# Values and two probability tiles per head turned by 32 x 32 blocks and a trip through memory, in a two-layer encoder kernel

## The chip, the cores and the metric

The kernel runs on one core of a Trainium2 chip. The metric is the device time of one launch in microseconds (us), the median of three runs. The engines are TensorE (PE, with its weight loads as PEld), VectorE (DVE), ScalarE (ACT), GpSimd (POOL) and SyncE (SP), which here only issues DMAs and waits for semaphores. HBM is called memory below.

## The reference, cut to what matters

Two layers of an encoder for 512 prompt tokens and 64 sample tokens with 128 cached ones. Layer 0 has sixteen heads: 0 to 7 ("mla") and 8 to 15 ("diff", two softmax maps a head). Layer 1 has eight, 16 to 23 ("dsa", over the keys that an indexer selects). Keys and values of the heads 8 to 23 are outputs too, one row a token.

```python
q_lat, kv_lat, kpe_raw, dq, dk, dv = jnp.split(h @ w_in, SPLIT_EVEN, axis=-1)
...
logits = jnp.einsum('bqhmd,bkhmd->bmhqk', q, k2) * DIFF_SCALE + bias
p = jax.nn.softmax(jnp.where(mask, logits, -jnp.inf), axis=-1)
attn = (p[:, 0] - lam * p[:, 1]).astype(v.dtype)
return jnp.einsum('bhqk,bkhd->bqhd', attn, v)
...
# layer 1: q, k, v of a head likewise; softmax over the selected keys, p @ v
return mixed @ w_out, new        # new: dk, dv (and k, v of layer 1) are returned
```

Everything is float32. A product is made of three matmuls of parts (high x high, high x low, low x high): ACT writes the high part of an operand, DVE or POOL the low one.

## The kernel before

Tokens lie along the free dimension: a projection gives a tile of 128 features x 576 tokens. Each engine runs its own program, written out by hand, and semaphores hold them together. `attention(h)` of every engine goes through the slots 0 to 7 of head `h`. In the slots 0 to 4 PE makes the scores of the query tiles t = 0 to 3 (128 queries, 128 (t + 1) keys) and of the sample (t = 4); all slots hold a share of the projections q, k and v of a later head (of h + 1, in layer 1 of h + 2) as k-tiles of six matmuls, and some hold tiles of the output projection of a finished pair of heads. The slots of such heads are long (heads 9, 11, 13, 19, 21 from slot 0, heads 8, 11, 13, 18, 20 from slot 4); heads 10, 12, 14 and 17 have none, and 22 and 23 have only such tiles.

- **Probabilities.** DVE adds bias to the scores (`row_maxima`), ACT exponentiates and scales, in a diff head DVE mixes both maps. In slot t + 2 PE turns the tile by t + 1 transposes into a bank of T (`turn_probs`), ACT takes the high part into PTh (`turned_hi`), DVE the low part into PTl (`turned_lo`).
- **Values.** In slot 1 PE turns the five tiles of values to tokens (`values_to_tokens`), DVE copies them into VF (`take_values`), SP stores VF as output in slot 4 (`store_keys`), ACT and POOL split it into Vh and Vl (`job("v", h)`, slot 4, for head 23 slot 3).
- **Keys** are stored in another way: DVE turns 32 x 32 blocks into KF (`take_keys`, in slot 7 of the head before), and eight DMAs (four quarters of the prompt, four of the sample) write runs of 32 floats to the output.
- **Weighted values.** `weighted_values(h - 1)` stands in slot 1 of head h, right behind the value transposes.

PE accumulates into pairs of banks (SHORT and LONG uses); a group may open when DVE has taken what was last in its pair. In an even diff head, the rows for a per-head norm go through the LONG pair in slot 7, and `b_norm` on DVE frees it; the next head's q begins in it. Weights come in units of 512 KB into four buffers: SP loads, ACT makes the high part, POOL (or DVE) the low one. SP issues all of it in one order: `load_next("slot", h, s)` at the end of every slot, and a DMA waits behind every wait ahead of it.

Of the kernel before, what the change touches and what calls it, by code (L numbers as in the profile page):

```python
# [30 lines left out]
P = 128  # L31
# [12 lines left out]
HEADS = 8  # L44
# [271 lines left out]
def build(nc, a, outs, scratch):  # L316
# [58 lines left out]
    def plan_attention(h):  # L375
# [5 lines left out]
        for s in range(SLOTS):  # L381
# [5 lines left out]
            if 2 <= s < 2 + TOK_TILES and (h, s) != (16, 6):  # L387
                tr.add("p", h, s - 2)
# [4 lines left out]
            if s == 1:  # L393
                tr.add("v", h)
                tr.add("v5", h)
                if h % 16:
                    group("pv", h - 1, use=SHORT)
# [324 lines left out]
    with ctx:  # L722
# [54 lines left out]
        RSTDQ = sb("RSTDQ", [P, NT])  # L777
        arena = cursor[0]
# [47 lines left out]
        assert e <= own  # L826
        (QIh, QIl), end3 = overlay(end3, ("QIh", [P, 4, NT], F32R), ("QIl", [P, 4, NT], F32R))
# [67 lines left out]
        keys_made = sem("keys_made")  # L895
# [12 lines left out]
        pt_hi = sem("pt_hi")  # L908
        b_sq, rb_sqrt = sem("b_sq"), sem("rb_sqrt")
# [115 lines left out]
        def _(sp):  # L1025
# [99 lines left out]
            def store_keys(g):  # L1125

                sp.wait_ge(keys_made, g - HEADS + 1)
                dst = ("diff_k", "dsa_k")[kind_of(g) == "dsa"]
                c = slice((g % HEADS) * HD, (g % HEADS + 1) * HD)
                for name, b0, b1 in (("_prompt", 0, SEQ // SQUARE), ("_sample", SEQ // SQUARE, NT // SQUARE)):  # L1130
                    tokens = outs[dst + name][:, c].rearrange("(b t) (q d) -> q t b d", t=SQUARE, d=SQUARE)
                    for q in range(QUADRANTS):
                        sp.dma_start(tokens[q], KF[q * SQUARE:(q + 1) * SQUARE, b0:b1, :]).then_inc(kf_out, 16)
                sp.wait_ge(t_free, tr.made("v5", g))
                dst = ("diff_v", "dsa_v")[kind_of(g) == "dsa"]
                sp.dma_start(outs[dst + "_prompt"][:, c].rearrange("(t p) d -> p t d", p=P), VF[:, 0:QT, :]).then_inc(vf_out, 16)
                sp.dma_start(outs[dst + "_sample"][:, c], VF[0:DEC, QT, :]).then_inc(vf_out, 16)

# [89 lines left out]
            sp.wait_ge(vf_out, 16 * 2 * 16)  # L1228
# [42 lines left out]
        def job_source(name):  # L1271

            w = name[0]
            if name == ("ckv", KLT - 1):
                return acc_free, acc.made("krow")
            if w in ("kpe", "ckv"):
                return lat_ready, jobs.made(*name)
            if w == "qi":
                return acc_free, acc.made(*name)
            g = name[1]  # L1280
            if w in ("q", "k") and g == 17:
                return y_made, Y_MADE[w]
# [145 lines left out]
        def _(pe):  # L1428
# [209 lines left out]
            def values_to_tokens(h):  # L1638
                out = rotate_to_tokens(("v", h))
                if h == 17:  # L1640
                    pe.wait_ge(y_made, Y_MADE["v"])
                else:
                    pe.wait_ge(acc_free, acc.made("v", h))
# [60 lines left out]

            def turn_probs(h, t):
# [83 lines left out]
            def attention(h):  # L1789
                g, x = prepared_in(h), next_head(h)  # L1790
                for s in range(SLOTS):
# [12 lines left out]
                    if 2 <= s < 2 + TOK_TILES and (h, s) != (16, 6):  # L1804
                        turn_probs(h, s - 2)
                    if s == 1:
                        values_to_tokens(h)
                        if h % 16:
                            weighted_values(h - 1)
# [392 lines left out]
        def _(act):  # L2202
# [123 lines left out]
            def exponents(h, t):  # L2326
                kind, r, w = kind_of(h), rows_of(t), keys_of(t)
                n = step_of(h, t)
                if n >= 2:
                    act.wait_ge(t_done, tr.made("p", *divmod(n - 2, TOK_TILES)))  # L2330
# [24 lines left out]

            def b_square(h):
# [11 lines left out]
            def attention(h):  # L2368
                g, x, p = prepared_in(h), next_head(h), finished_pair(h)
                for s in range(SLOTS):  # L2370
# [6 lines left out]
                    if 2 <= s < 2 + TOK_TILES and (h, s) not in ((15, 5), (16, 4)):  # L2377
                        turned_hi(h, s - 2)
# [411 lines left out]
        def _(dve):  # L2790
# [235 lines left out]

            def take_values(h):
# [3 lines left out]
                if h > 8:  # L3031
                    dve.wait_ge(vf_out, 16 * 2 * stored_before(h))
# [45 lines left out]
            def mix_maps(h, t):  # L3078
# [5 lines left out]
                                         op0=ALU.mult, op1=ALU.add).then_inc(p_mixed, 1)  # L3084

# [72 lines left out]
            def attention(h):  # L3158
                g, x, p = prepared_in(h), next_head(h), finished_pair(h)
                for s in range(SLOTS):  # L3160
# [3 lines left out]
                    if s < TOK_TILES:  # L3164
                        row_maxima(h, s)
                    if h == 16 and s < 3:
# [6 lines left out]
                    if s == 1 and h != 16:  # L3173
# [5 lines left out]
                    if 2 <= s < 2 + TOK_TILES:  # L3179
                        turned_lo(h, s - 2)  # L3180
                    if s == 4 and h in (10, 12, 14, 15):
# [260 lines left out]
            def ffn(layer):  # L3442
# [4 lines left out]
                dve.wait_ge(vf_out, 16 * 2 * HEADS * (layer + 1))  # L3447
# [581 lines left out]
```

## Time and profile before

| | |
|---|---|
| median of three runs | 1642.27 us (1641.88 to 1643.78) |
| profiled execution | 1643.9 us, of it the span 1642.1 us |
| PE, PEld busy | 98%, 95% |
| DVE, ACT, POOL busy | 73%, 55%, 55% |
| share of the 16 DMA engines, main queue | 30.1% |
| granted PE clock, mean | 0.997 |
| stretch of heads 8 to 15 | from 263.8 us |
| stretch of heads 16 to 23 | from 1016.2 us |

Times in the trace are microseconds from the start of the span. The busy share of PE is high because matmuls are pipelined and overlap in the records: what an instruction costs is the distance from its start to the next one's. An engine's idle time costs only where another waits for it.

### The profile page before, as it was taken

To read this page: it belongs to the slowest core of one execution; us is meant where nothing else is said; L and a number is where in the kernel's file an instruction comes from. 1 tells how busy PE (TensorE), PEld (TensorE's weight loads), DVE (VectorE), ACT (ScalarE), POOL (GpSimd) and SP (SyncE) were. 2 spreads that over 40 slices of the span, in tenths; PEclk is the share of its full clock that TensorE was granted. 3 is DMA by queue.
4 is the path that set the end of the run, shared out by engine and by line. 5 is a ranking of instruction groups with operands and counts; after the bars stand their busy time and mean duration, and the time that the engine had idled before them with its cause. 6 is when DMAs were issued, how large, how long until landed. Compare 5 with 4: busy or idle time off the path is not lost.

```text
span 1642.1 us, 32437 instructions
## 1 busy us (share of the span) xinstructions
PE 1612.4 (98%) x12028; PEld 1563.2 (95%) x12028; DVE 1202.8 (73%) x2233; ACT 902.5 (55%) x1776; POOL 903.1 (55%) x703
## 2 busy tenths in 40 slices
PE   9999999999999999999999999999999999999998
PEld 8989999999999999999999999899999999999997
DVE  5666655656656799889897789634357998898977
ACT  4365545454546665565565445644367655655654
POOL 4453445364544067677575547664450676775754
PEclk9999999999999999999999999999999999999999
DMA  6221223343422223423323332344242233233232
GB/s 189 81 64 53 67 78 86 77 108 77 112 75 68 65 78 92 115 71 111 97 84 90 89 81 70 92 120 110 64 110 60 78 94 112 74 107 98 84 91 71
DMA packets 283008, 145.50 MB, mean 89 GB/s; under 512 B 60591, under 2 KB 273261, under 8 KB 282853
## 3 DMA queue, kind: packets, MB, share of 16 engines
q1 hardware_dynamic: 278392, 136.27, 30.1%
q0 software_dynamic: 3616, 6.92, 1.6%
q8 instruction: 98, 1.61, 0.4%
q14 instruction: 58, 0.47, 0.1%
q10 hardware_dynamic: 844, 0.24, 0.1%
HBM read 130.69 MB, written 15.32 MB: 89 GB/s over the span
## 4 chain that ended last, share of the span: by engine, by line
PE 81%; DVE 11%; ACT 3%; issue 3%; POOL 1%; DMA 0%; POOLq 0%; ACTq 0%; DVEq 0%
PE ACC L1444 29%; PE ACC L1883 11%; PE ACC L1884 11%; PE ACC L1885 11%; PE ACC L1724 2%; PE S L1699 2%; PE S L1885 2%; PE S L1883 2%; PE S L1884 2%; DVE SCO L3137 2%; DVE TOP L3134 1%; PE T L1444 1%; ACT PR L2335 1%; PE T L1712 1%; PE S L1673 1%
## 5 line engine op out<-in xcount | busy, mean ns | idle before, releaser
L3645 POOL TENSOR_TENSOR WL<-RAW,WH 128x1024 fp32r<-128x1024 f32 (+3 forms) x89 | 187.8, 2114 | 147.2 <-ACT WH L2210 147.0
L1444 PE MATMUL ACC<-XGh,WH 128*128 128x288 f32 (+1 forms) x1008 | 227.6, 307 | 6.3 <-DVE XGl L2828 1.8
L1444 PE MATMUL ACC<-XGh,WL 128*128 128x288 f32 (+1 forms) x1008 | 215.3, 295 | 0.0
L1444 PE MATMUL ACC<-XGl,WH 128*128 128x288 f32 (+1 forms) x1008 | 215.3, 295 | 0.0
L1883 PE MATMUL ACC<-TB,WH 128*128 128x288 f32 x640 | 188.5, 295 | 1.4 <-DVE TB L3355 1.4
L1885 PE MATMUL ACC<-TB,WL 128*128 128x288 f32 x640 | 188.6, 295 | 0.0
L1884 PE MATMUL ACC<-TB,WH 128*128 128x288 f32 x640 | 188.3, 294 | 0.0
L2493 ACT ACTIVATE TC<-ACC 128x288 f32<-128x288 f32 x192 | 79.0, 411 | 167.7 <-PE ACC L1885 167.0
L1444 PEld LDWEIGHTS ACC<-XGh,WH 128*128 128x128 f32 (+1 forms) x1008 | 159.0, 188 | 11.4 <-issue 4.0
L1444 PEld LDWEIGHTS ACC<-XGh,WL 128*128 128x128 f32 (+1 forms) x1008 | 161.6, 188 | 0.0
L1444 PEld LDWEIGHTS ACC<-XGl,WH 128*128 128x128 f32 (+1 forms) x1008 | 161.3, 187 | 0.0
L2335 ACT ACTIVATE PR<-SX,STAT 128x128 f32<-128x128 f32 (+4 forms) x160 | 85.7, 536 | 119.4 <-DVE STAT L3065 117.6
L2822 DVE TENSOR_TENSOR X<-ACC,X 128x576 f32<-128x576 f32 x89 | 66.7, 753 | 83.8 <-PE ACC L1444 79.4
L2210 ACT ACTIVATE WH<-RAW 128x1024 fp32r<-128x1024 f32 (+4 forms) x127 | 116.3, 923 | 12.9 <-PE S L1444 4.5
L1883 PEld LDWEIGHTS ACC<-TB,WH 128*128 128x128 f32 x640 | 120.2, 188 | 1.8 <-issue 1.8
L3308 DVE TENSOR_TENSOR WL<-RAW,WH 128x512 fp32r<-128x512 f32 (+3 forms) x128 | 120.4, 941 | 2.0 <-ACT WH L2511 2.0
L1884 PEld LDWEIGHTS ACC<-TB,WH 128*128 128x128 f32 x640 | 120.5, 188 | 0.0
L1885 PEld LDWEIGHTS ACC<-TB,WL 128*128 128x128 f32 x640 | 120.3, 188 | 0.0
L2511 ACT ACTIVATE WH<-RAW 128x1024 fp32r<-128x1024 f32 (+3 forms) x128 | 100.5, 787 | 34.4 <-PE S L1885 34.4
L3652 POOL TENSOR_TENSOR Ql<-YQ,Qh 128x576 fp32r<-128x576 f32 x24 | 34.9, 1455 | 112.2 <-ACT Qh L2241 112.1
L2351 ACT ACTIVATE PTh<-T 128x128 fp32r<-128x128 f32 (+1 forms) x96 | 41.2, 429 | 99.1 <-PE T L1712 98.8
L1883 PE MATMUL ACC<-XGh,WH 128*128 128x288 f32 x320 | 94.3, 295 | 0.0
(517 smaller groups left out, 5244.2 us busy)
## 6 DMA issues: line engine op xcount, KB each, us to landing
RAW<-in_w_gate_dram SPq DMA_DIRECT2D x44, 512.0 KB, 3.9
RAW<-in_w_up_dram SPq DMA_DIRECT2D x44, 512.0 KB, 5.0
RAW<-in_w_down_dram SPq DMA_DIRECT2D x48, 384.0 KB, 3.8
RAW<-in_w_in_even_dram SPq DMA_DIRECT2D x29, 512.0 KB, 5.2
RAW<-in_w_in_odd_dram SPq DMA_DIRECT2D x28, 512.0 KB, 4.6
RAW<-in_w_out_even_dram SPq DMA_DIRECT2D x16, 512.0 KB, 4.2
RAW<-in_w_down_dram SPq DMA_DIRECT2D x16, 256.0 KB, 2.9
RAW<-in_w_out_odd_dram SPq DMA_DIRECT2D x8, 512.0 KB, 5.1
```

Source lines behind the costliest of these rows:

```text
L1444: ins = pe.matmul(out[0:m, 512 * b:512 * b + width], left, right[:, b * width:(b + 1) * width], start=(first and part == 0), stop=(last an ...
L1883: pe.matmul(out, hi[:, w], xh, start=first and k == 0, stop=False, skip_group_check=not first)
L1884: pe.matmul(out, hi[:, w], xl, start=False, stop=False, skip_group_check=not first)
L1885: ins = pe.matmul(out, lo[:, w], xh, start=False, stop=k == count - 1, skip_group_check=not first)
L2210: act.activation(WH[slot][:, 0:n], RAW[slot][:, 0:n], ACT.Copy).then_inc(w_hi, 1)
L2335: act.activation(PR[m][0:r, n % 2, 0:w], SX[m][0:r, 0:w], ACT.Exp, bias=STAT[0:r, n % 2, m:m + 1], scale=-1.0, accum_out=STAT[0:r, n % 2, ...
L2351: act.activation(PTh[:, 0:t + 1, t * P:(t + 1) * P], out[:, 0:(t + 1) * P].rearrange("p (j q) -> p j q", q=P), ACT.Copy).then_inc(pt_hi, 1)
L2493: act.activation(dst, sum_bank(j), ACT.Copy).then_inc(copy_done, 1)
L2511: act.activation(blocks_of(layer, what, w)[0], src, ACT.Copy).then_inc(s7_hi, 1)
L2822: return lambda out: dve.tensor_tensor(two(X[:, m, :]), halves(out), two(X[:, m, :]), ALU.add)
L3308: dve.tensor_tensor(lo, src, hi.bitcast(F32), ALU.subtract).then_inc(s7_lo, 1)
L3645: pool.tensor_tensor(WL[slot][:, 0:n], RAW[slot][:, 0:n], WH[slot][:, 0:n].bitcast(F32), ALU.subtract).then_inc(w_lo_pool, 1)
```

## The change

Values of the heads 8 to 15 and 17 to 23 (`blockwise`) are no more turned by PE. DVE turns their 32 x 32 blocks into VT (`turn_values`, slot 0, for head 17 slot 1), SP stores VT by eight DMAs as it does the keys (slot 4 of its order, right behind them), waits after slot 7 until they have landed, and loads the stored output back into VF by two DMAs (`load_values`); `job("v", h)` waits for that.

The probability tiles t = 2 and 3 of the heads 8 to 14 and 17 to 22 (`BLOCK_HEADS`) are no more turned by PE either: DVE turns their blocks into PB (`probs_to_blocks`, slot t + 1), SP writes PB in four DMAs to a place in the memory of y_prompt and loads it back turned, by one DMA into PF (`turn_through_memory`, after `load_values`; between tile 2 and tile 3 stand the weight loads of slot 0 of the next head). ACT and DVE split PF (`loaded_hi`, `loaded_lo`: tile 2 in the slots 5 and 6, tile 3 in slot 7 of both, on DVE ahead of `b_norm` and of the end of v's projection). `weighted_values(h)` waits for the last of them.

Where slot 1 has an unfinished projection (the heads 9 to 14 and 17 to 21), `weighted_values(h - 1)` now stands behind the first of its three k-tiles (`values_late`).

```diff
+BLOCK_TILES = (2, 3)
+BLOCK_HEADS = (8, 9, 10, 11, 12, 13, 14, 17, 18, 19, 20, 21, 22)
...
+                if blockwise(g):
+                    sp.wait_ge(vals_made, value_loads(g) // 32 + 1)
+                    for name, b0, b1 in (("_prompt", 0, SEQ // SQUARE), ("_sample", SEQ // SQUARE, NT // SQUARE)):
+                        tokens = outs[dst + name][:, c].rearrange("(b t) (q d) -> q t b d", t=SQUARE, d=SQUARE)
+                        for q in range(QUADRANTS):
+                            sp.dma_start(tokens[q], VT[q * SQUARE:(q + 1) * SQUARE, b0:b1, :]).then_inc(vf_out, 16)
+                    return
...
+            def load_values(g):
+                sp.wait_ge(vf_out, value_stores(g + 1))
+                sp.wait_ge(job_lo, jobs.made("v", g - 1))
...
+            def store_blocks(h, t):
+                b = BLOCK_HEADS.index(h)
+                sp.wait_ge(pb_made, block_number(h, t) + 1)
+                if b:
+                    sp.wait_ge(pf_in[t], 16 * b)
+                place, first = turned_place(t)
+                for q in range(QUADRANTS):
+                    dst = bass.AP(place, first + q * SQUARE, [[P, SQUARE], [P * SQUARE, QUADRANTS * (t + 1)], [1, SQUARE]])
...
+            def load_turned(h, t):
+                b = BLOCK_HEADS.index(h)
+                sp.wait_ge(pb_out[t], 16 * QUADRANTS * (b + 1))
...
+            def turn_through_memory(h):
+                store_blocks(h, 2)
+                load_turned(h, 2)
+                load_next("slot", h + 1, 0)
+                store_blocks(h, 3)
+                load_turned(h, 3)
...
-                    load_next("slot", h, s)
+                    if s or h - 1 not in BLOCK_HEADS:
+                        load_next("slot", h, s)
+                if blockwise(h):
+                    load_values(h)
+                if h in BLOCK_HEADS:
+                    turn_through_memory(h)
...
+                if h in BLOCK_HEADS:
+                    pe.wait_ge(pf_lo, block_number(h, BLOCK_TILES[-1]) + 1)
...
+                    elif s == 1 and values_late(h):
+                        prepare(*c[:2], c[2], c[2] + 1)
+                        weighted_values(h - 1)
+                        prepare(*c[:2], c[2] + 1, c[3])
...
+            def loaded_hi(h, t):
+                act.wait_ge(pf_in[t], 16 * (BLOCK_HEADS.index(h) + 1))
+                act.wait_ge(acc_done, acc.made("pv", h - 1))
+                act.activation(PTh[:, 0:t + 1, t * P:(t + 1) * P], PF[t][:, :, :],
+                               ACT.Copy).then_inc(pf_hi, 1)
...
+            def turn_values(g):
+                if g > 8:
+                    dve.wait_ge(vf_out, value_stores(g))
+                dve.transpose(VT[:, :, :].rearrange("p b d -> p (b d)"), raw_values(g)[:, 0:NT]).then_inc(vals_made, 1)
...
+            def probs_to_blocks(h, t):
+                w = (t + 1) * P
+                dve.transpose(PB[t][:, 0:w], PR[0][:, n % 2, 0:w]).then_inc(pb_made, 1)
...
+            def loaded_lo(h, t):
+                dve.wait_ge(pf_hi, block_number(h, t) + 1)
+                dve.tensor_tensor(PTl[:, 0:t + 1, cols], PF[t][:, :, :],
+                                  PTh[:, 0:t + 1, cols].bitcast(F32), ALU.subtract).then_inc(pf_lo, 1)
```

## Rows read from the trace of the kernel before

**Rows 1.** The page, busy us, share of the span and instructions of each engine.

```profile
PE 1612.4 (98%) x12028; PEld 1563.2 (95%) x12028; DVE 1202.8 (73%) x2233; ACT 902.5 (55%) x1776; POOL 903.1 (55%) x703
```

**Rows 2.** Waits of PE, heads 8 to 15: us in total, times, longest.

```profile
PE ACC L1444 <- DVE YQ L2989: 1.3, 4, 0.7
```

**Rows 3.** Timeline of PE: start us, us to the end of the last.

```profile
285.67 0.60 PE L1712 MATMUL T<-IDN,PR 128*128 128x128 f32 x4
286.03 0.50 PE L1444 MATMUL ACC<-XGh,WH 128*128 128x288 f32 x2
286.37 0.42 PE L1444 MATMUL ACC<-XGl,WH 128*128 128x288 f32 x2
286.63 0.43 PE L1444 MATMUL ACC<-XGh,WL 128*128 128x288 f32 x2
...
304.46 0.66 PE L1645 MATMUL T<-IDN,YV 128*128 128x128 f32 x4
...
304.98 0.48 PE L1724 MATMUL ACC<-PTh,Vh 128*128 128x512 f32 x1
```

**Rows 4.** The instruction of a block transpose of keys: ns min/median/max, starts.

```profile
L3022 DVE STREAM_TRANSPOSE KF<-YK x16: 765/768/773, 261.2 to 1217.2; 128x576 f32<-128x576 f32 x16
```

**Rows 5.** Timeline of SP: key stores of the heads 15, 17 and 22.

```profile
505.03 1.98 SPq L1133 DMA_DIRECT2D out_diff_k_prompt_dram<-KF  x4
507.05 1.93 SPq L1133 DMA_DIRECT2D out_diff_k_sample_dram<-KF  x4
...
1050.34 3.11 SPq L1133 DMA_DIRECT2D out_dsa_k_sample_dram<-KF  x4
...
1201.98 3.21 SPq L1133 DMA_DIRECT2D out_dsa_k_sample_dram<-KF  x4
```

**Rows 6.** Head 15's four prompt stores of keys (505 to 507): issue to landing.

```profile
DMA to landing us min/median/max: 1.8/2.0/2.0
```

**Rows 7.** The same for head 18, 0.9 us behind a weight load.

```profile
L1133 SPq DMA_DIRECT2D out_dsa_k_prompt_dram<-KF x4: 344/536/2198, 1068.3 to 1069.8; - x4
DMA to landing us min/median/max: 3.7/3.8/4.1
```

**Rows 8.** Two 512 KB weight loads issued at 308.0 and 308.7: issue to landing.

```profile
DMA to landing us min/median/max: 4.8/5.4/6.0
```

**Rows 9.** DMA issues: count, KB each, median us to landing.

```profile
MH<-bias_tiles POOLq DMA_DIRECT2D x16, 224.0 KB, 2.9
out_diff_k_sample_dram<-KF SPq DMA_DIRECT2D x32, 8.0 KB, 1.8
```

**Rows 10.** Timeline of DVE in head 10: the last of row_maxima(10, 3), and b_norm(9).

```profile
349.48 0.08 DVE L3065 DVE_READ_ACCUMULATOR2_ANT STAT<- 128x1 f32 x1
...
363.06 0.81 DVE L3114 SCALAR_TENSOR_TENSOR BO<-BO,GSUB,ACC 128x576 f32<-128x576 f32 x1 [0.55 <-PE ACC L1459]
```

**Rows 11.** Timeline of PE: scores (11, 0) and (18, 1), weighted values of 22 and 23.

```profile
364.55 0.33 PE L1673 MATMUL S<-Kh,Qh 64*128 64x128 f32 x2
...
1072.66 0.28 PE L1699 MATMUL S<-Kh,Qh 128*128 128x256 f32 x1
...
1219.13 0.48 PE L1724 MATMUL ACC<-PTh,Vh 128*128 128x512 f32 x1
...
1233.07 0.39 PE L1724 MATMUL S<-PTh,Vh 128*128 128x512 f32 x1
```

**Rows 12.** Timelines of ACT and DVE in head 23.

```profile
1227.58 0.83 ACT L2241 ACTIVATE Vh<-VF 128x768 fp32r<-128x768 f32 x1
...
1230.73 0.58 ACT L2351 ACTIVATE PTh<-T 128x512 fp32r<-128x512 f32 x1
...
1231.34 0.69 DVE L3090 TENSOR_TENSOR PTl<-T,PTh 128x512 fp32r<-128x512 f32 x1 [0.50 <-ACT PTh L2351]
```

**Rows 13.** Windows: busy us of each engine (instructions), PE clock, DMA share, GB/s.

```profile
535.00:540.00 5.00, 3.75 (x27) 3.22 (x26) 1.35 (x5) 1.65 (x5) 0.38 (x1) 0.97 0.20 61
540.00:545.00 5.00, 5.00 (x28) 5.00 (x28) 1.39 (x2) 1.51 (x2) 1.18 (x2) 0.69 0.02 3
```

More of the change, by code:

```diff
@@ L148, in early_output, with blockwise, value_stores, value_loads @@
     return h - 1 if h % 2 and kind_of(h) == "dsa" else None
+def blockwise(g):
+    return kind_of(g) != "mla" and g != 16
+def value_stores(g):
+    return 16 * sum(2 * QUADRANTS if blockwise(i) else 2 for i in range(8, g))
+def value_loads(g):
+    return 16 * 2 * sum(blockwise(i) for i in range(8, g))
+BLOCK_TILES = (2, 3)
+BLOCK_HEADS = (8, 9, 10, 11, 12, 13, 14, 17, 18, 19, 20, 21, 22)
+def in_blocks(h, t):
+    return h in BLOCK_HEADS and t in BLOCK_TILES
+def block_number(h, t):
+    return BLOCK_HEADS.index(h) * len(BLOCK_TILES) + BLOCK_TILES.index(t)
 def q_job_slot(g):
@@ L386, in plan_attention @@
                     scores(("s", h, s, m), m if k == "diff" else s % 2)
-            if 2 <= s < 2 + TOK_TILES and (h, s) != (16, 6):
+            if 2 <= s < 2 + TOK_TILES and (h, s) != (16, 6) and not in_blocks(h, s - 2):
                 tr.add("p", h, s - 2)
@@ L393, in plan_attention @@
             if s == 1:
-                tr.add("v", h)
-                tr.add("v5", h)
+                if not blockwise(h):
+                    tr.add("v", h)
+                    tr.add("v5", h)
                 if h % 16:
@@ L1284, in job_source @@
                 return acc_free, acc.made(w, g)
+            if w == "v" and blockwise(g):
+                return vf_in, value_loads(g + 1)
             if w == "v":
@@ L1639, in values_to_tokens @@
                 out = rotate_to_tokens(("v", h))
[L1640 to L1643, printed above, removed]
+                pe.wait_ge(acc_free, acc.made("v", h))
                 for t in range(QT):
@@ L1703, in head_scores, with values_late @@
                     ins.then_inc(s_done, 1)
+            def values_late(h):
+                c = share(h, 1)
+                return h > 8 and blockwise(h) and c is not None and c[3] < c[4]
             def turn_probs(h, t):
@@ L2329, in exponents @@
                 if n >= 2:
-                    act.wait_ge(t_done, tr.made("p", *divmod(n - 2, TOK_TILES)))
+                    before = divmod(n - 2, TOK_TILES)
+                    if in_blocks(*before):
+                        act.wait_ge(pb_made, block_number(*before) + 1)
+                    else:
+                        act.wait_ge(t_done, tr.made("p", *before))
                 if h == 16 and t == 0:
@@ L2376, in attention @@
                         job("k", g)
-                    if 2 <= s < 2 + TOK_TILES and (h, s) not in ((15, 5), (16, 4)):
+                    if 2 <= s < 2 + TOK_TILES and (h, s) not in ((15, 5), (16, 4)) and not in_blocks(h, s - 2):
                         turned_hi(h, s - 2)
@@ L2427, in attention @@
                         cached_keys_hi(x)
+                    if s == 7 and h in BLOCK_HEADS:
+                        loaded_hi(h, 3)
                     if (h, s) != (16, 2):
@@ L3165, in attention @@
                         row_maxima(h, s)
+                    if s and in_blocks(h, s - 1):
+                        probs_to_blocks(h, s - 1)
                     if h == 16 and s < 3:
@@ L3172, in attention @@
                         take_keys(h)
-                    if s == 1 and h != 16:
+                    if s == (1 if h == 17 else 0) and blockwise(h):
+                        turn_values(h)
+                    if s == 1 and not blockwise(h) and h != 16:
                         take_values(h)
@@ L3178, in attention @@
                         evacuate(("wo", *out_tile(h, s)), add_to_x(out_tile(h, s)[1]))
-                    if 2 <= s < 2 + TOK_TILES:
+                    if 2 <= s < 2 + TOK_TILES and not in_blocks(h, s - 2):
                         turned_lo(h, s - 2)
+                    if s == 6 and h in BLOCK_HEADS:
+                        loaded_lo(h, 2)
                     if s == 4 and h in (10, 12, 14, 15):
@@ L3210, in attention @@
                         take_keys(x)
+                    if s == 7 and h in BLOCK_HEADS:
+                        loaded_lo(h, 3)
                     if s == 7:
```

51 lines of the change are left out of this document (41 added, 10 removed).

## The prediction

> **What bounds the kernel now.** I read the page's first part, then the waits of PE, then PE's timeline through heads 8 to 23, and last SP's, DVE's and ACT's beside it. PE is busy 98% of the span; DVE, which gets the new transposes, 73% [rows 1]. In the stretch of the diff heads PE's longest item of waiting is 1.3 us in all [rows 2]. So PE sets the time there: an instruction taken off PE gives back its distance to the next start, and every wait put on PE is paid in full. The timeline of PE shows what a transpose costs: not the 272 ns of its record, but the step to the next start [rows 3]. SP's timeline shows how long its order is: the key stores occupy it some 4 to 5.5 us a head [rows 5], and what is new is nearly all behind them.
>
> **What is removed.** Value transposes: from the first of the five to the next matmul 0.52 us (304.46 to 304.98) [rows 3]. Of the 15 heads that lose them, 13 (8 to 15, 17 to 21) count here: 6.8 us. Those of 22 and 23 lie in a stretch that the memory trips will set (below). Probability tiles: four transposes take 0.36 us, and the first pair of matmuls behind them 0.34 where the steady pair after it takes 0.26 (286.37 to 286.63), so 0.44 us for t = 3 and three quarters of it, 0.33, for t = 2 [rows 3]. 0.77 us in 12 heads (8 to 14, 17 to 21) is 9.2 us. Weighted values inside a projection mean one more switch from long matmuls to others, 0.08 us by the same rows, in 11 heads: 0.9 us back. **Saved on PE: 15.1 us.**
>
> **What hides, and behind what.** DVE loses two copies of values and gets blocks of 384 and 512 columns: by 0.77 us for 576 columns [rows 4] 0.51 and 0.68 us. With the values' 0.77 that is 2.0 us a head; it lies under DVE's 27% of idle time [rows 1] and costs nothing as long as it comes ahead of a free bank; ACT's and DVE's splits stay, only their source moves. In long-slot heads the trips hide too: from the block to the split PE has 18 us of work there. What must be counted is SP's order in the heads with short slots.
>
> **The price of a trip.** No row shows these DMAs; the key stores have the same shape (four DMAs, 128 byte runs, 256 KB). Nothing ahead of them: four issued in 1.98 us, the last 1.5 us after the first, landing 2.0 later: 3.5 us [rows 5, 6]. Behind one weight load: last issued at 1069.8, landing 3.7 later, 1073.5 less 1068.3 is 5.2 [rows 7]. Two loads back to back land 0.7 + 6.0 = 6.7 us after the first issue [rows 8], and stores behind them then need some 2.0 more. The load back, 256 KB in 512 byte runs: 2.9 us as the bias load of 224 KB [rows 9], not under the 2.0 of [rows 6]. Splits: ACT 0.6, DVE 0.7, so 1.3 [rows 12]. Issuing a load takes SP 0.4 to 0.6.
>
> The Trainium skill (DMA: Bandwidth & Descriptors, Anatomy of one DMA) puts a DMA at 2.0 us fixed plus bytes by 436 GB/s. It gives 2.6 us for the load back, an estimate, and 3.65 for a group of stores, against 3.5 to 5.2 in [rows 6, 7]; it knows nothing of what stands ahead in the queue, which the second row does show.
>
> **Heads 10 and 12.** Tile 2's block is made at 349.5 + 0.55 = 350.1 [rows 10]. Stores 3.5: SP waits until 353.6; load 0.4; then two weight loads (slot 0 of heads 11 and 13), and tile 3's stores only behind them, landing at 354.0 + 6.7 + 2.0 = 362.7; load 2.9, splits 1.3: 366.9. Only then does DVE do `b_norm(9)`, 0.8: 367.7, where it ended at 363.9 [rows 10]. PE wants that bank behind the scores of (11, 0), at 364.55 + 0.45 - 0.76 = 364.2 [rows 11]. Stall 3.5 us, twice: 7.0. With stores at 3.5 whatever is ahead it would be 363.7, no stall; with all at the high rows 6 each. **Head 14** has one weight load between: 354.6 + 5.2 + 2.9 + 1.3 + 0.8 = 364.8, 0.6 late, and the first output tile behind it waits for the split of the same b_norm: I take 1.4. The odd heads have no b_norm there and get through.
>
> **Head 17.** Keys are out at 1053.5 [rows 5]; eight value stores 4.5 (between 3.9 and 5.5 of the key rows), the weight load 0.6 in their landing of 1.8 [rows 9]: 1059.8; value loads 0.9; tile 2's stores 4.4 (half way between 3.5 and 5.2), load and weight load 1.0, tile 3's stores behind it 5.2, load 2.9, splits 1.3, then v's evacuation 0.8: 1076.3. PE wants the weighted values a k-tile (0.8) behind the scores of (18, 1): 1072.66 - 1.28 + 0.45 + 0.8 = 1072.6 [rows 11]. Stall 3.7 (0 by the low rows, 6 by the high).
>
> **Heads 22 and 23.** All slots of 22 are short, and its whole queue must pass. Keys out at 1205.2 [rows 5]; value stores 4.5, landing 1.8, value loads 0.9, stores 4.4, load and weight load 1.0, stores 4.4, load 2.9, splits 1.3: 1226.4, where weighted_values(22) began at 1219.13 [rows 11]. And head 23's values queue behind that: SP free at 1222.6, keys 4.5, value stores from 1227.6 (DVE turns them only behind the split) 4.5, landing 1.8, value loads 2.9: 1236.8, where ACT took Vh at 1227.58 [rows 12]. What follows Vh up to the last weighted values (5.5 us to 1233.07 [rows 11, 12]) is ACT's own order and moves along. **9.2 us** at the end of the layer; 4.5 by the lowest rows of each term, 16 by the highest.
>
> **The clock.** The one stretch with a low granted clock stands behind a window in which PE worked 3.75 of 5 us; it lost 0.03 and 0.31 of 5 us, 1.7 us [rows 13]. In head 23 PE would now stand still for 7 us, so I add the same once: 1.7 (0 to 3.4). That is the step from 2.4 to 1.2 GHz. The Trainium skill (TensorE: Matmul & The Clock Gate, What's actually happening) too says that idleness halves the clock; the sum stands on the row.
>
> **Sum.** -15.1 + 7.0 + 1.4 + 3.7 + 9.2 + 1.7 = +7.9 us on the span of 1642.1. The profiled execution took 1643.9, 1.6 above the median; set on the median 1642.3 that is 1650.2.
>
> **The rivals.**
> 1. *The trips come late* (forecast): 1650.2; its own range 1646 to 1661. For it: the additions above take the middle of measured rows, and in head 22 even the lowest leave 4.5 us.
> 2. *What is ahead in the queue does not count* (the other side). Each group of stores takes 3.5 us, each load 2.9. Then heads 10, 12 and 14 wait for nothing, 17 for 1.1, the end moves by 7.4, the clock by 1.7: -15.1 + 10.2 = -4.9, 1637.4; with the shortest rows and no drop of the clock -15.1 + 4.5, 1631.7. It decides from the point where all waits together stay under 11.8 us. For it: the small stores may pass the big loads; against it [rows 7]. The DMA page's rule above is this rival's: by it the stalls are 0, about 1 and some 8 us, 1638 or so.
> 3. *Gain and waits meet*: the waits sum to 11.8 to 18.4 us, 1642.3 within 3.3. That is, one of heads 10/12 or 17 gets through, and the end costs 7.
> 4. *The late trips spread.* `job("v", h)` waits for values that come back behind weight loads, ACT stands in slot 4 (17 and 22 surely, for 2.5 us), the next head's exponents and blocks are later, and even heads with long slots pay. With all terms at their high ends: -15.1 + 12 + 4 + 6 + 16 + 3.4 = +26, 1668.
> That the change does not do what it says I exclude: nothing else turns these tiles.
>
> **How the numbers follow.** Chances: (1) 0.50, (2) 0.24, (3) 0.17, (4) 0.09. Three launches of this kernel lie within 0.12%, so 0.2% (3.3 us) is what can be told. (1) and (4), with a small tail of (3), are slower: 0.60; (3) the same: 0.17; (2) faster: 0.23. The range leaves out the far half of (4) and the low third of (2): 1633 to 1662.
>
> **What would show it.** PE's transposes gone: 166 fewer of 128 columns, and no value group in slot 1. DVE: 15 transposes from YV, 26 into PB. In the waits of PE, DVE's PTl in slot 1 of 23 and 18, BO of b_norm in slot 0 of 11 and 13. SP: tile 3's stores of head 10 issued at some 5 us behind tile 2's; landing of them by far above 2.0. The trip of 22 done some 7 us after PE wants it, and Vh of 23 some 9 late against the head's start. The forecast is wrong if the stores behind two weight loads land in 4 us, or if the sequence of SP in head 22 takes less than 14 us from the last key store to the split.

## The result and the profile after

| | before | after |
|---|---|---|
| median of four launches, us | 1642.2 (1641.9 to 1643.8) | 1655.5 (1653.2 to 1656.8) |
| ratio to before | | 1.0077 (1.006 to 1.0095, 95%) |
| span of the profiled execution, us | 1642.1 | 1653.7 |

The change makes the kernel slower by 0.8%. 1650.2 was forecast, in a range of 1633 to 1662. The first part of the page after, against [rows 1]:

```profile
PE 1603.6 (97%) x11854; PEld 1552.9 (94%) x11862; DVE 1232.2 (75%) x2244; ACT 903.7 (55%) x1776; POOL 905.3 (55%) x703
```

PEld has 166 instructions fewer, the number reckoned (PE's own records are 174 fewer; the profile lacks a few of them), and PE is busy 8.8 us less, yet the span grew by 11.6 us. Busy time hides why: an instruction at the lower clock is busy for longer. So I cut each span into windows of 2 us and sum over them: **standing** (length less PE's busy time), **clock** (busy time times one less the granted clock) and **work** (the rest, PE's work at full clock). All three come from the columns of the windows view.

| us | standing | clock | work | span |
|---|---|---|---|---|
| before | 29.7 | 2.5 | 1609.9 | 1642.1 |
| after | 50.1 | 10.0 | 1593.6 | 1653.7 |
| difference | +20.4 | +7.5 | -16.3 | +11.6 |

The saving on PE came as reckoned. It bought 20.4 us of standing and, beside it, 7.5 us at the lower clock.

**Where PE stands.** The longest groups in the view of PE's waits, heads 8 to 15 and then 17 to 23, against the 1.3 us of [rows 2]:

```profile
PE ACC L1542 <- DVE BO L3259: 4.8, 2, 2.7
PE T L1815 <- DVE PR L3212: 2.0, 4, 1.2
PE ACC L1542 <- DVE YV L3110: 1.3, 2, 1.0
PE S L1768 <- DVE STAT L3194: 1.3, 2, 1.1
...
PE ACC L1542 <- DVE X L2943: 5.0, 1, 5.0
PE ACC L1826 <- DVE YV L3110: 3.6, 2, 3.2
PE ACC L1826 <- DVE PTl L3228: 1.1, 1, 1.1
```

L1542 is the matmul of all projections, L1826 that of the weighted values, L3259 is `b_norm` (the two waits are in slot 0 of heads 11 and 13), L3110 frees v's bank (the long wait is in head 18), L2943 is the addition of an output tile to X at the end of head 22. None of these three works on probabilities: each is queued on DVE behind the split of a loaded tile. Head 10's trip of tile 3 on SP's timeline, the landing of its four stores (the view of that line), then ACT, DVE and PE:

```profile
348.76 2.67 SPq L1209 DMA_DIRECT2D out_y_prompt_dram<-PB  x4
352.82 0.40 SPq L1219 DMA_DIRECT2D PF<-out_y_prompt_dram  x1
353.26 0.49 SPq L1132 DMA_DIRECT2D RAW<-in_w_in_even_dram  x1
353.79 0.58 SPq L1132 DMA_DIRECT2D RAW<-in_w_out_even_dram  x1
354.47 3.26 SPq L1209 DMA_DIRECT2D out_y_prompt_dram<-PB  x4
361.43 0.40 SPq L1219 DMA_DIRECT2D PF<-out_y_prompt_dram  x1
...
DMA to landing us min/median/max: 4.4/5.0/5.1
...
364.11 0.63 ACT L2470 ACTIVATE PTh<-PF 128x512 fp32r<-128x512 f32 x1 [4.47 <-DMA PF<-out_y_prompt_dram]
364.77 0.69 DVE L3228 TENSOR_TENSOR PTl<-PF,PTh 128x512 fp32r<-128x512 f32 x1 [3.82 <-ACT PTh L2470]
365.38 0.81 DVE L3259 SCALAR_TENSOR_TENSOR BO<-BO,GSUB,ACC 128x576 f32<-128x576 f32 x1
...
362.99 0.33 PE L1768 MATMUL S<-Kh,Qh 64*128 64x128 f32 x2
...
366.24 0.85 PE L1542 MATMUL ACC<-XGh,WH 128*128 128x288 f32 x2 [2.71 <-DVE BO L3259]
...
367.37 0.68 PE L1542 MATMUL ACC<-XGh,WL 128*128 128x288 f32 x2
367.85 0.68 PE L1542 MATMUL ACC<-XGh,WH 128*128 128x288 f32 x2
```

The stores stand behind two weight loads and land 5.0 us after issue, the load back follows at 361.43, the split ends at 365.5, `b_norm` at 366.2, and PE has stood for 2.71 us. The reader is to see the last rows too: the pairs of 288 columns now start 0.48 us apart, where they stood 0.26 apart in [rows 3]. The windows view of the same stretch (columns as in [rows 13]):

```profile
364.00:366.00 2.00, 0.00 (x0) 0.00 (x0) 1.23 (x2) 1.20 (x2) 0.61 (x1) 0.86 0.90 236
366.00:368.00 2.00, 1.76 (x7) 1.76 (x8) 1.96 (x7) 1.55 (x2) 1.81 (x2) 0.50 0.96 160
368.00:370.00 2.00, 2.00 (x10) 2.00 (x9) 0.38 (x2) 1.76 (x7) 0.41 (x1) 0.50 0.07 11
370.00:372.00 2.00, 2.00 (x10) 2.00 (x10) 0.00 (x0) 1.84 (x2) 1.03 (x1) 0.50 0.48 72
```

The clock is at its lower level, 1.2 of 2.4 GHz, behind the standing, and 3.0 us of work are lost to it: the wait cost some twice its length. The same is found behind the wait of head 13 (1.5 us lost), that of 18 (1.6) and in head 23 (4.2).

**By head.** From the first scores of a head to those of the next (the end: to the last weighted values of head 23), from PE's timelines, with the step of the forecast beside it:

| us | before | after | moved by | forecast |
|---|---|---|---|---|
| heads 8 and 9 | 71.0 | 70.0 | -1.0 | -2.5 |
| 10 and 11 | 71.2 | 75.4 | +4.2 | +1.1 |
| 12 and 13 | 71.2 | 72.7 | +1.5 | +1.1 |
| 17 and 18 | 59.7 | 61.9 | +2.2 | +1.3 |
| 19 to 21 | 98.9 | 95.5 | -3.4 | -3.6 |
| 22 and the end | 31.4 | 40.3 | +8.9 | +10.9, with the clock |

### The profile page after: what moved, and what is told of

It is laid out like the page before. It is cut to its first block, busy times and chain, and to the rows that moved or that the text cites. A ratio compares the mean times of both kernels' runs of the same rounds, so it can differ in the third digit from the quotient of the medians.

```text
span 1653.7 us, 32416 instructions
## 1 busy us (share of the span) xinstructions
PE 1603.6 (97%) x11854; PEld 1552.9 (94%) x11862; DVE 1232.2 (75%) x2244; ACT 903.7 (55%) x1776; POOL 905.3 (55%) x703
## 4 chain that ended last, share of the span: by engine, by line
PE 71%; DVE 13%; DMA 4%; issue 4%; ACT 3%; SPq 3%; POOL 1%; DVEq 0%; POOLq 0%; ACTq 0%
PE ACC L1542 22%; PE ACC L1990 11%; PE ACC L1991 11%; PE ACC L1992 11%; DMA out_y_prompt_dram<-PB 2%; PE ACC L1826 2%; PE S L1992 2%; PE S L1990 2%; PE S L1991 2%; PE S L1794 2%; DVE SCO L3282 2%; DMA PF<-out_y_prompt_dram 2%; SPq L1209 1%; DVE TOP L3279 1%; PE T L1542 1%
## 5 line engine op out<-in xcount | busy, mean ns | idle before, releaser
L1542 PE MATMUL ACC<-XGh,WH 128*128 128x288 f32 (+1 forms) x1008 | 228.5, 308 | 11.5 <-DVE BO L3259 4.8
L1542 PE MATMUL ACC<-XGh,WL 128*128 128x288 f32 (+1 forms) x1008 | 216.7, 297 | 0.0
L1542 PE MATMUL ACC<-XGl,WH 128*128 128x288 f32 (+1 forms) x1008 | 216.5, 296 | 0.0
L1542 PEld LDWEIGHTS ACC<-XGh,WH 128*128 128x128 f32 (+1 forms) x1008 | 160.4, 190 | 18.6 <-DVE BO L3259 5.1
L1542 PEld LDWEIGHTS ACC<-XGh,WL 128*128 128x128 f32 (+1 forms) x1008 | 162.7, 189 | 0.0
L1542 PEld LDWEIGHTS ACC<-XGl,WH 128*128 128x128 f32 (+1 forms) x1008 | 162.6, 189 | 0.0
L2943 DVE TENSOR_TENSOR X<-ACC,X 128x576 f32<-128x576 f32 x89 | 66.6, 752 | 79.2 <-PE ACC L1542 75.0
L1992 PE MATMUL ACC<-XGh,WL 128*128 128x288 f32 x320 | 94.3, 295 | 0.0
```

Of the source, the lines that this page charges most:

```text
L1542: ins = pe.matmul(out[0:m, 512 * b:512 * b + width], left, right[:, b * width:(b + 1) * width], start=(first and part == 0), stop=(last an ...
L1992: ins = pe.matmul(out, lo[:, w], xh, start=False, stop=k == count - 1, skip_group_check=not first)
L2943: return lambda out: dve.tensor_tensor(two(X[:, m, :]), halves(out), two(X[:, m, :]), ALU.add)
```

## The experiments

Each ran in turns with the kernel before, which lay at 1642.8 to 1643.6 (median) in the four groups, its launches within 3.6 to 6.3 us of each other in a group. Some kernels spread more, and the spread goes with the clock: norm first's launches run from 1646.6 at a mean granted clock of 0.996 to 1654.8 at 0.992. So the table of heads stands beside the medians. It is from one profiled execution each, and for norm first and filled waits that one is the slowest of six (1654.8 and 1665.9). Every column but the median and its ratio is from that execution; the last four are heads.

| kernel | median | ratio (95%) | standing | clock | work | 10, 11 | 12, 13 | 18 | 22, end |
|---|---|---|---|---|---|---|---|---|---|
| before | 1642.2 | | 29.7 | 2.5 | 1609.9 | 71.2 | 71.2 | 32.8 | 31.4 |
| after | 1655.5 | 1.0077 | 50.1 | 10.0 | 1593.6 | 75.4 | 72.7 | 36.4 | 40.3 |
| values only | 1642.3 | 0.9998 (0.999 to 1.0007) | 34.1 | 3.3 | 1602.4 | 70.7 | 70.7 | 32.3 | 35.5 |
| tiles only | 1653.3 | 1.0069 (1.0053 to 1.0085) | 44.7 | 3.2 | 1601.8 | 75.2 | 72.4 | 33.0 | 36.7 |
| hidden heads | 1636.6 | 0.996 (0.9949 to 0.9972) | 35.1 | 3.1 | 1597.4 | 70.3 | 70.0 | 31.6 | 31.4 |
| norm first | 1650.3 | 1.0045 (1.003 to 1.006) | 49.7 | 9.9 | 1593.4 | 71.1 | 73.0 | 36.7 | 44.5 |
| trips first | 1648.5 | 1.0026 (1.0017 to 1.0036) | 46.2 | 8.6 | 1593.4 | 71.2 | 70.9 | 38.1 | 38.7 |
| waits in before | 1660.3 | 1.0093 (1.0078 to 1.0108) | 39.8 | 8.4 | 1609.3 | | | | |
| late splits | 1639.4 | 0.9966 (0.9954 to 0.9978) | 39.4 | 1.4 | 1596.2 | 70.2 | 70.2 | 31.6 | 34.2 |
| filled waits | 1659.2 | 1.0087 (1.0063 to 1.0111) | 52.6 | 12.4 | 1599.0 | | | | |
| POOL splits | 1642.9 | 0.9997 (0.9988 to 1.0006) | 38.4 | 4.7 | 1597.7 | | | | |
| late, trips first | 1634.1 | 0.9951 (0.9938 to 0.9965) | 34.2 | 1.5 | 1596.6 | 70.2 | 70.3 | 31.6 | 31.4 |
| the same, POOL | 1641.3 | 0.9987 (0.9978 to 0.9996) | 39.0 | 4.2 | 1596.3 | | | | |
| POOL in layer 0 | 1632.7 | 0.9936 (0.9922 to 0.995) | 33.9 | 0.0 | 1597.0 | 69.8 | 69.8 | 31.6 | 31.4 |

**1. Values only.**

```diff
-BLOCK_HEADS = (8, 9, 10, 11, 12, 13, 14, 17, 18, 19, 20, 21, 22)
+BLOCK_HEADS = ()
```

> Values in blocks as in the changed kernel, every probability tile turned on PE again. Theory A (the probability trips make the waits of heads 10 to 17; the value trips cost something only at the layer's end, where eight stores stand between head 23's keys and its values and Vh comes back late): 15 heads save 7.8 us, the switch takes 0.9, the end waits some 4.5 and loses 1.5 of clock: 1641, between 1638 and 1643; no wait of PE in slot 0 of heads 11 and 13 or in slot 1 of 18. Rival B (value trips are hidden everywhere): 1635. Rival C (the eight value stores on SP's queue are what delays everything): above 1645.

Theory A holds, B and C fall: 7.5 us of work are saved, no wait above 0.5 us appears in heads 10 to 21, and the end takes 4.1 us of it back (35.5 against 31.4). There ACT stood for the loaded values, and PE for the exponents queued behind:

```profile
1224.13 0.84 ACT L2348 ACTIVATE Vh<-VF 128x768 fp32r<-128x768 f32 x1 [1.66 <-DMA VF<-out_dsa_v_sample_dram]
...
1226.63 0.41 PE L1815 MATMUL T<-IDN,PR 128*128 128x128 f32 x2 [1.81 <-ACT PR L2454]
```

**2. Tiles only.**

```diff
 def blockwise(g):
-    return kind_of(g) != "mla" and g != 16
+    return False
...
```

> Probability tiles in blocks as in the changed kernel, all values turned on PE. Theory A: the waits in slot 0 of 11 and 13 stay, with their clock (9 us together), the wait of slot 1 of head 18 goes (its trip starts 6 us earlier), head 22's trip ends some 3 us earlier: about 1651, 1647 to 1654. Rival C (value stores are the chief delay): the waits go with them, 1642.2 - 9.5 plus some 3, near 1636. Rival D (a wait of PE costs only its own length): 1645.

Not shown: waits that the turning of values on PE needs again. Theory A holds (1653.3, in its 1647 to 1654), though of its two drops of the clock only the one in head 11 came (1.7 us lost; behind the 1.85 us in head 13 the clock stayed). Heads 10 to 13 lose what they lose with the whole change, so that loss is the tiles'. Head 18 is at 33.0, where it is at 32.3 with values only and at 36.4 with both: its wait needs both, eight value stores ahead of a trip. At the end the parts nearly add up (4.1 and 5.3 against 8.9 for both).

**3. Only the heads with long slots.** Tiles in 10, 12, 14, 17 and 22, and the values of 22 and 23, go back to PE.

```diff
-BLOCK_HEADS = (8, 9, 10, 11, 12, 13, 14, 17, 18, 19, 20, 21, 22)
+BLOCK_HEADS = (8, 9, 11, 13, 18, 19, 20, 21)
-    return kind_of(g) != "mla" and g != 16
+    return kind_of(g) != "mla" and g not in (16, 22, 23)
...
```

> Tiles in blocks only in heads 8, 9, 11, 13 and 18 to 21, whose trips were found without a wait of PE behind them; values in blocks in all but 16, 22 and 23. Theory A (the gain per transpose is there, and the loss sits in heads 10, 12, 14, 17, 22 and 23 alone): 8 times 0.77 and 13 times 0.52 less 0.9 is 12 us, 1630, between 1627 and 1633, granted clock 0.997 or more. Rival E (the queue's added load is paid a little in every head): 1636 to 1642.

All long waits go, and the kernel is 0.4% faster than before. The time is rival E's. Work fell by 12.5 us as theory A had it, but standing rose by 5.4. Of this 4.0 lie in the heads 8 to 22, in waits of 0.2 to 1.2 us for DVE in heads 8 to 11, 13, 17 and 20; 1.2 lie behind the last head, where the kernels are alike and their executions differ by as much. So the forecast's "costs nothing" for DVE's new work was wrong by some 4 us.

**4. The norm ahead of the split on DVE.** In slot 7, `b_norm` is put above `loaded_lo(h, 3)`.

> One change to the changed kernel: in slot 7, DVE does the normalisation of the finished pair (which frees PE's bank) ahead of the split of the loaded tile 3. Theory A (the bank waits only because it is queued behind the split, and each of those waits brings a stretch at half clock): the waits of 2.7 and 2.1 us in slot 0 of 11 and 13 go, and with them 4.5 us of clock: 1655.5 - 9.3 = 1646, 1644 to 1648. Rival D (a wait costs its length only): 1650.5. Rival F (weighted values of 10 and 12 then wait for the split instead): above 1652.

Half of it. Heads 10 and 11 fall from 75.4 to 71.1, but 12 and 13 do not, and the median fell by 5.2 where 9.3 were expected. The median of 1650.3 is the number of rival D, but not for its reason: in the profiled execution the clock fell behind a wait of 1.62 us in head 13 and took 1.7 us, and at the end of the layer it took 6.7. The two fastest launches, 1646.6 and 1647.6 at a mean clock of 0.996, lie where theory A had it. In heads 12 and 13 the wait changed its name: ACT too has an order, with the high split ahead of the output job whose MIXh and MIXl PE wants next:

```profile
363.39 0.63 ACT L2470 ACTIVATE PTh<-PF 128x512 fp32r<-128x512 f32 x1 [4.58 <-DMA PF<-out_y_prompt_dram]
363.93 1.25 ACT L2348 ACTIVATE MIXh<-BO 128x576 fp32r<-128x576 f32 x2
...
437.72 0.51 PE L1542 MATMUL ACC<-MIXh,WH 128*128 128x288 f32 x2 [1.62 <-POOL MIXl L3805]
```

**5. Both trips ahead of the weight loads.**

```diff
     load_turned(h, 2)
-    load_next("slot", h + 1, 0)
     store_blocks(h, 3)
     load_turned(h, 3)
+    load_next("slot", h + 1, 0)
```

> One change to the changed kernel: SP issues the weight loads of the next head's slot 0 behind the whole trip of tile 3, not between the two trips. Theory A (the weight loads ahead in the queue are what makes tile 3's stores of head 10 land 5.0 us after their issue): they land in 2 to 2.5 us, the load back is issued near 357.9 instead of 361.4, and the waits of slot 0 of heads 11 and 13 go with their clock; the trip of head 22 ends some 2.5 us earlier; 1655.5 less 9 less 3 is 1643.5, and up to 5 us worse where weights, now 4 to 5 us later, come too late themselves. Rival 2 (what stands ahead does not count): stores land in 5 us again, the trip starts 1.2 us earlier and that is all: 1653.

The landing of head 10's four stores of tile 3, where it was 5.0:

```profile
DMA to landing us min/median/max: 2.0/2.2/2.3
```

Rival 2 falls: what stands ahead in the queue is 2.8 us of that landing of 5.0. The load back went out at 356.04, and of the waits in heads 11 and 13 some 0.8 us each is left, at full clock. The whole gained 7.0 us of the 12 expected: head 18 waits as before (3.29) and lost more to the clock (3.1).

**6. Waits made in the kernel before.** Copies into an unused tile `DL`, each behind the one before, ahead of the norm.

```diff
 for b in rows_in(h, s):
+    for _ in range({10: 2, 12: 5, 14: 8}.get(h, 0)):
...
+        dve.tensor_copy(DL[:, :], BO[:, b % 2, :]).then_inc(delayed, 1)
...
     b_norm(b)
```

> The kernel before, nothing turned in memory, with copies of BO into an unused tile put on DVE ahead of the normalisation in slot 7: two in head 10, five in head 12, eight in head 14 (0.67 us each). PE then waits some 1.0, 3.0 and 5.0 us in slot 0 of heads 11, 13 and 15. Theory A (a wait of PE of 2 us and more brings a stretch at half clock behind it, whatever it waits for): 9.0 of waiting and 3 to 6 of clock, 1654 to 1658, with 0.50 behind the second and third wait and 1.00 behind the first. Rival D (the half clock of the changed kernel has another cause, such as the transfers or the changed order on PE): granted clock 1.00 in these stretches, 1651.

The waits were 2.47, 3.95 and 3.69 us, other sizes than meant, 10.1 in all; so the control, a short wait with the clock left at 1.00, is missing, and the median of 1660.3 lies above theory A's range. The windows behind the second:

```profile
443.35 0.85 PE L1446 MATMUL ACC<-XGh,WH 128*128 128x288 f32 x2 [3.95 <-DVE BO L3116]
...
443.00:445.00 2.00, 1.65 (x7) 1.66 (x8) 1.38 (x6) 1.44 (x2) 0.91 (x1) 0.50 0.00 0
445.00:447.00 2.00, 2.00 (x10) 2.00 (x10) 0.38 (x2) 1.75 (x7) 0.50 (x1) 0.50 0.00 0
```

Rival D falls: no block, no trip, hardly a transfer (DMA share 0.00 here, at most 0.06 behind the other two waits), and the clock stands at 0.50 behind all three. Standing grew by 10.1 and clock by 5.9, the span by 15.4.

**7. Late splits.** Hidden heads and 10, 12, 14; in both layers `loaded_hi(h, 3)` last in the head on ACT, `loaded_lo(h, 3)` last in slot 7 on DVE.

> As the kernel of hidden heads (tiles in blocks in 8, 9, 11, 13, 18 to 21, values in all but 16, 22, 23), and heads 10, 12 and 14 in blocks again, with the split of tile 3 put last in the head on ACT (behind both output jobs) and last in slot 7 on DVE (behind the normalisation, the weights' split and the output tile). Theory A (in these heads nothing but the order behind the waiting split cost time): 1636.6 less 3 times 0.77 is 1634.3, no wait above 1.2 us. Rival F (another instruction behind the split, or the weighted values, waits instead): 1638 or more, with a new wait of PE in heads 11 or 13.

In layer 0 no long wait is left, but heads 10 to 14 are only 0.1 us shorter than with hidden heads, for six tiles more (2.3 expected): what PE saves there it waits for in pieces of up to 0.9 us. In layer 1 the late split of head 21 comes too late for head 22's short slots (a wait of 2.59). 1639.4: a place in an order that is free in one head is taken in another.

**8. Filled waits.** The scores ahead of the waits are made again and again; the last time alone signals. Not shown: those of (18, 1), six times in the same way.

```diff
+repeats = {(11, 0): 7, (13, 0): 6}.get((h, t), 1)
+for again in range(repeats):
     for i, (left, right) in enumerate(((qh, Kh), (qh, Kl), (ql, Kh))):
...
```

> The changed kernel with useless work on PE where it stood still: the scores of (11, 0) made seven times, those of (13, 0) and (18, 1) six times, each into its own bank with the same result. It fills some 2.7, 2.2 and 2.5 us of waits of 2.7, 2.1 and 3.2. Theory A (the half clock comes from PE standing still): these three stretches stay at 1.00 and 4 to 6 us of clock are given back: 1650 to 1651.5, faster by more work. Rival D (the clock has another cause): 1655.5, and 0.50 in these stretches as before.

A miss: 1659.2 for 1650 to 1651.5. In the profiled execution, the slowest of six, the tile of head 10 itself came back 1.4 us later (its load took 4.0 us where it had taken 2.7), so PE stood 2.31 us behind the added work and the clock fell all the same; head 18 likewise (2.48), and new waits of 2.65 and 3.60 us stand in heads 15 and 22. The launches run from 1651.5 at a mean clock of 0.997 to 1665.9 at 0.991. Only head 13 gives the reading that was meant: 0.77 us of standing left in that wait, clock 1.00, and the head no longer (43.4 against 43.6) for 2 us of added work. One instance shows little; that PE's standing brings the lower clock rests on experiment 6.

**9 to 12. What is left of the small waits, and a faster kernel.** In 9 and 11 `loaded_lo` moves to POOL; 10 is 7 with `h < 16` for the late splits and for the order of 5 on SP; 11 is 10 with POOL; 12 has POOL in layer 0 alone.

> The kernel of hidden heads (1636.6), with the 16 low splits of loaded tiles moved from DVE to POOL. On DVE these take 0.67 to 4.4 us (median 1.3) where the same split from PSUM takes 0.54 and 0.69, the long ones while POOL works. Theory G (the small waits of PE that came in, 4.2 us over 8 heads, are DVE running late behind these splits): they fall by half or more, 1634 to 1635. Rival H (they come from what PE reaches earlier with a chain of ACT and DVE that is no shorter; the split is not in it): 1636 to 1637. Rival I (POOL's splits come late and hold its weights' splits): above 1638.

> Hidden heads and 10, 12, 14 in blocks; for layer 0 the trips stand ahead of the next head's weight loads on SP and the splits of tile 3 stand last on ACT and DVE; layer 1 as in hidden heads. Theory A (the two parts of the loss in heads 10 and 12 are the queue ahead of tile 3's stores and the order behind the waiting split; with both gone the pairs 10 and 11, 12 and 13 lose their small waits of 0.4 to 0.9 us): 1636.6 less 2 is 1634.5. Rival H (PE's gain there is capped by the chain of ACT and DVE): 1636 to 1637, no wait above 1.2 us. Rival I (later weight loads hold PE): above 1638 with waits for WL.

> The kernel before in this list with its 22 low splits on POOL. Theory G: another 1 to 2 us less than that kernel, 1633. Rival H: the same time as it. Rival I: slower than it.

> The fastest kernel so far (1634.1), with the low splits of loaded tiles on POOL in layer 0 alone, where the two kernels that had them there showed heads 10 to 13 shorter by 0.4 us a pair, and on DVE in layer 1, where POOL's came late (3.9 us of waiting in head 22). Theory G2 (POOL has time for them in layer 0 only): 1634.1 less 0.8, 1633.3, no new wait in heads 20 and 22. Rival H: 1634.1, no difference that can be told. Rival I2 (POOL's order costs elsewhere in layer 0): above 1635.

9 and 11 go rival I's way in time. In layer 1 POOL's own order holds the split back until PE has waited 3.9 us in head 22:

```profile
1194.98 2.35 POOL L3789 TENSOR_TENSOR WL<-RAW,WH 128x1024 fp32r<-128x1024 f32 x1
1197.28 1.26 POOL L3892 TENSOR_TENSOR PTl<-PF,PTh 128x512 fp32r<-128x512 f32 x1
...
1198.80 0.76 PE L1826 MATMUL ACC<-PTh,Vh 128*128 128x512 f32 x1 [3.88 <-POOL PTl L3892]
```

In layer 0, where POOL is in time, 9 goes rival H's way: against hidden heads the same waits stand in heads 8, 9, 11, 13 and 17, and PE's standing in heads 8 to 14 is only 0.2 us less (4.8 for 5.1, before 2.3).

10 came out where theory A had it (1634.1 for 1634.5; its interval overlaps that of hidden heads), but not for its reason: the pairs 10 to 13 are as long as in 7. Against hidden heads the profiled execution is shorter by 1.2 and 0.7 us in heads 17 and 20, which 10 does not change and where waits of 0.9 and 0.5 us are there in some kernels' executions and not in others; why was not found out. It is shorter by another 1.1 us from head 15 to the end of layer 0, where the clock fell in the execution of hidden heads (3.1 us lost) and did not in that of 10. 12 makes each of those pairs 0.4 us shorter and is the fastest, 0.64% under the kernel before, at 1632.7 for 1633.3 expected.

## Why the prediction was near, and what was off

**Right: the price of the trips.** Head 10: 8.6 us from one load back to the other (9.1 forecast), 2.7 for the load (2.9), splits 1.3; the waits in heads 11 and 13 are 2.7 and 2.1 (3.5 each). The rule for one DMA that the prediction takes from the Trainium skill (DMA: Bandwidth & Descriptors, Anatomy of one DMA) stands in that section for DMAs that POOL issues, and these are SP's; it made 2.6 us of that load, an estimate. The wait put down to head 17's trip is 3.2 (3.7), head 15's, behind `b_norm(13)`, 1.0 and 0.5 (1.4). At the end, less the 2.1 us by which head 22 starts later: weighted values of 22 at 1226.0 (1226.4), Vh of 23 at 1236.4 (1236.8), the last weighted values at 1241.9 (1242.3). One link was missing: PE stood first, for 5.04 us, on the output tile of head 22, which DVE had queued behind the split of tile 2.

```profile
1221.19 0.97 DVE L3228 TENSOR_TENSOR PTl<-PF,PTh 128x384 fp32r<-128x384 f32 x1
1222.09 1.41 DVE L2943 TENSOR_TENSOR X<-ACC,X 128x576 f32<-128x576 f32 x2
...
1222.88 0.85 PE L1542 MATMUL ACC<-MIXh,WH 128*128 128x288 f32 x2 [5.04 <-DVE X L2943]
1228.09 0.77 PE L1826 MATMUL ACC<-PTh,Vh 128*128 128x512 f32 x1 [1.08 <-DVE PTl L3228]
```

The agreement of Vh has luck in it. The values of head 23 landed at 1236.9, which less 2.1 is 1234.8 and 2.0 us sooner than forecast, and ACT took them only at 1238.5, without a wait for them:

```profile
1234.45 0.48 SPq L1195 DMA_DIRECT2D VF<-out_dsa_v_sample_dram  x1
...
DMA to landing us min/median/max: 2.5/2.7/2.9
...
1237.89 0.72 ACT L2454 ACTIVATE PR<-PR,STAT 128x512 f32<-128x512 f32 x1 [0.23 <-DVE STAT L3202]
1238.52 0.83 ACT L2348 ACTIVATE Vh<-VF 128x768 fp32r<-128x768 f32 x1
```

ACT had to finish the exponents of tile 3 first, whose scores PE made late: from 1228.1 to 1232.4 PE was at work without a stop at half clock, which is 2.1 us lost. In norm first the lower clock lasted longer there (to 1234.7), the values landed at 1234.4, and Vh started at 1238.1, 3.7 us later; in trips first it ended sooner, and Vh waited 0.91 us for the values.

**Right: the saving.** 16.3 us of work; 15.1 were counted, and 1.8 more in heads 22 and 23 by the same prices.

**Wrong: the clock, charged "once" and in head 23 alone.** There the 1.7 us are about right, though not as they were worked out: 4.2 us of work were lost, 2.1 of them ahead of a wait that swallowed them (1.08 us were left of it) and 0.5 more before the values landed, so that by this reckoning some 1.6 us reached the end. It was left out behind the waits of heads 11, 13 and 18, where nothing swallows it and the lower clock took 3.0, 1.5 and 1.6 us: 6.1 us, more than the whole miss of the sum. In return the dip of [rows 13] (1.6 us) is not there in the profiled execution after. That is chance: it stands behind a wait of 1.17 us at the end of layer 0 that all fourteen profiled executions have, and behind which the clock fell in five. [rows 13] showed a dip behind a window in which PE stood for only 1.25 of 5 us; I had read it as an event of one place.

**Wrong: DVE's 2.0 us a head "costs nothing".** Heads 8 and 9 kept 1.0 of their 2.5 us, and hidden heads shows 4.0 us of standing more in the heads 8 to 22 with no trip late. Most of it in layer 0 is not the splits, since experiment 9 took them from DVE and the waits stayed: I take it that PE comes sooner to a point where the chain of ACT and DVE is no shorter, which no run shows by itself. Part is a term I had at nothing, that "only their source moves", in the view of tile PTl:

```profile
L3235 DVE TENSOR_TENSOR PTl<-T,PTh x70: 244/386/693, 88.1 to 1242.3; 128x128 fp32r<-128x128 f32 x24, 128x256 fp32r<-128x256 f32 x24, 128x384 fp32r<-128x384 f32 x11, 128x512 fp32r<-128x512 f32 x11
L3228 DVE TENSOR_TENSOR PTl<-PF,PTh x26: 666/1289/4402, 289.3 to 1227.1; 128x384 fp32r<-128x384 f32 x13, 128x512 fp32r<-128x512 f32 x13
```

With the late splits of 10 this part counts: POOL's taking them shortened heads 10 to 13 by 0.8 us in 12. In layer 1 the division was not settled.

**The sum.** By head, what was missed: ahead of 8 -0.2, 8 and 9 +1.5, 10 to 13 +3.5, 14 and 15 with the dip -1.0, 17 to 21 +1.2, the end -2.0, behind the layer +0.6, which with the rounding is 3.7 us over the forecast's +7.9. So the time came out near partly because the clock left out (+6.1) met a dip that did not come, a shorter trip of values and shorter waits. Rival 2 is refuted by experiment 5, as [rows 7] had spoken against it; standing alone passed its deciding sum of 11.8 us by 8.6, and rival 3's upper end of 18.4 too. Of rival 4 little is seen: ACT stood 2.4 us for the values in head 22, and PE then 0.56 for the exponents.

## What to carry to other kernels

A wait of some 2 us and more on the engine that sets the time may cost its length again at the lower clock (2.7 and 3.0 us in head 11), less what a later wait swallows of it (2.6 of 4.2 us at the end of the layer). When work moves from one engine to a round trip, look past the consumer: the waiting split stands in two in-order queues, and it is the innocent instruction behind it (a norm, an evacuation, an addition) that stops PE. Such a trip pays in the heads whose slots cover it and is best left out of the others: eleven heads with their own order gave -0.6%, all thirteen +0.8%.

## What the runs showed of the hardware

**Waits and clock.** In the profiled executions of all kernels, heads 8 to 23, the lower clock stands behind each of the fifteen longest waits of PE (2.71 to 5.55 us). Shorter ones went both ways: behind 1.62, 1.81, 2.13, 2.31, 2.47, 2.48 and 2.65 it fell, behind 1.85 and 2.59 it did not, and behind the 1.17 us that all fourteen have at the end of layer 0 it fell in five and not in nine. So the length of the last wait does not decide alone; what else does, no run here was made to show. A drop cost 1.5 to 6.7 us. The Trainium skill (TensorE: Matmul & The Clock Gate, HAM oscillation — how this bites in real kernels) describes a kernel that starts each tile at the lower clock after waiting for its DMA; the rows agree in kind. That the same wait may or may not bring a drop goes with the scatter of the launches: norm first over 8.2 us, the fastest kernel, with no wait above 1.2, over 1.1. It is not the rule, for the kernel before has no longer wait either and scatters over 3.6 to 6.3 us.

**DVE beside POOL.** The same subtraction takes at most 0.69 us with one source in PSUM and up to 4.40 with both in SBUF. The longest, and what POOL did meanwhile:

```profile
1139.34 4.40 DVE L3228 TENSOR_TENSOR PTl<-PF,PTh 128x512 fp32r<-128x512 f32 x1 [1.22 <-ACT PTh L2470]
...
1139.40 1.43 POOL L3805 TENSOR_TENSOR Ql<-YQ,Qh 128x576 fp32r<-128x576 f32 x1
1140.79 2.39 POOL L3798 TENSOR_TENSOR WL<-RAW,WH 128x1024 fp32r<-128x1024 f32 x1
```

It ends 0.6 us behind POOL's two. The other splits are alike. In 20 of the 26, one of POOL's own subtractions was under way when the split began, or began within 0.1 us, and the split ended 0.41 to 0.42 us (384 columns) or 0.55 to 0.56 us (512) behind the end of one. In five POOL had none beside them until their last 0.1 us, and 128x512 took 0.69; one took 1.27 beside three DMA issues of POOL. The Trainium skill (GPSIMD Engine Reference, Specifications) says that POOL shares its SBUF interfaces with VectorE, in contention with instructions that have two SBUF inputs; the trace agrees. The block transposes have one input and keep their time, in the view of tile PB near the 0.51 and 0.68 us of the forecast:

```profile
L3222 DVE STREAM_TRANSPOSE PB<-PR x26: 571/638/711, 279.6 to 1212.5; 128x384 f32<-128x384 f32 x13, 128x512 f32<-128x512 f32 x13
```
